# Projecting the keys of two heads at once, from rounded parts, in a latent attention kernel

## What is computed

```python
def mla(q_lat, kv_lat, k_rope, positions, q_norm_g, w_qb, kv_norm_g, w_kvb):
    q = (rms_norm(q_lat, q_norm_g) @ w_qb).reshape(bsz, s, MLA_HEADS, QK_NOPE + QK_ROPE)
    kv = (rms_norm(kv_lat, kv_norm_g) @ w_kvb).reshape(bsz, s, MLA_HEADS, QK_NOPE + V_HEAD)
    k_nope, v = kv[..., :QK_NOPE], kv[..., QK_NOPE:]
    ...
    k_pe = apply_rope(k_rope, cos, sin)
    ...
    k_full = jnp.concatenate([k_nope, jnp.broadcast_to(k_pe[:, :, None, :], ...)], axis=-1)
    out = causal_attention(q_full, k_full, v)
```

## Time and profile before

| | us |
|---|---|
| median of 3 runs (2299.27 to 2305.75) | 2302.62 |
| profiled execution, its own time | 2304.09 |
| span of that execution, first to last instruction | 2302.1 |
| TensorE busy | 2217.9 |
| VectorE busy | 1410.8 |
| GpSimd busy | 1114.1 |
| ScalarE busy | 960.9 |

### The profile page before, as it was taken

The page is one execution under the profiler, slowest core; times in us unless marked ns, Lnnn a source line. Parts: engine busy times, 40 slices in busy tenths (PEclk is TensorE's granted clock), DMA queues, the critical chain, the costliest instruction groups (busy, mean ns, idle before and its releaser), DMA issues.

```text
span 2302.1 us, 29018 instructions
## 1 busy us (share of the span) xinstructions
PE 2217.9 (96%) x10159; PEld 1806.5 (78%) x10159; DVE 1410.8 (61%) x2088; ACT 960.9 (42%) x1725; POOL 1114.1 (48%) x753
## 2 busy tenths in 40 slices
PE   8999999999999999999999999999999999999997
PEld 6786777878788888778888878878777888877886
DVE  6956655257666667697651115663876767677855
ACT  5636555124444444434531114451444444453343
POOL 2314333424577777544634322224346777764442
PEclk9999999999999999999999999999999999999998
DMA  5100000302132322664321110021123222238332
GB/s 180 46 19 1 1 0 28 128 28 97 69 119 88 111 95 81 238 199 115 92 103 62 46 37 28 28 101 55 31 84 119 87 115 84 111 136 292 95 94 91
DMA packets 66303, 203.34 MB, mean 88 GB/s; under 512 B 7360, under 2 KB 7488, under 8 KB 63104
## 3 DMA queue, kind: packets, MB, share of 16 engines
q1 hardware_dynamic: 63296, 187.19, 23.8%
q10 hardware_dynamic: 2880, 14.49, 1.6%
HBM read 152.89 MB, written 48.76 MB: 88 GB/s over the span
## 4 chain that ended last, share of the span: by engine, by line
PE 63%; DVE 14%; POOL 11%; ACT 5%; issue 5%; DMA 1%; ACTq 0%; POOLq 0%; SPq 0%; DVEq 0%
PE ps L853 9%; PE ps L855 9%; PE ps L854 9%; PE ps L985 6%; PE ps L989 6%; PE ps L987 6%; POOL wlo L644 5%; DVE ps L1226 4%; ACT ps L1043 2%; PE ps L1635 2%; POOL piece L653 2%; POOL stage L655 2%; POOL s_tmp L659 2%; DVE ps L1228 2%; PE ps L920 1%
## 5 line engine op out<-in xcount | busy, mean ns | idle before, releaser
L853 PE MATMUL ps<-ahi,whi 128*128 128x512 f32 x960 | 394.7, 411 | 14.1 <-DVE alo L2354 9.9
L566 POOL TENSOR_TENSOR whi<-stage,cons 128x1024 fp32r<-128x1024 f32 x64 | 125.3, 1958 | 527.3 <-PE ps L855 321.3
L855 PE MATMUL ps<-ahi,wlo 128*128 128x512 f32 x960 | 376.9, 393 | 0.0
L854 PE MATMUL ps<-alo,whi 128*128 128x512 f32 x960 | 376.9, 393 | 0.0
L644 POOL TENSOR_TENSOR wlo<-stage,whi 128x512 fp32r<-128x512 f32 x144 | 193.9, 1358 | 177.5 <-ACT whi L1086 177.5
L644 POOL TENSOR_TENSOR wlo<-A,whi 128x512 fp32r<-128x512 f32 x132 | 180.8, 1373 | 198.6 <-ACT whi L1096 198.6
L985 PE MATMUL ps<-x_hi,whi 128*128 128x512 f32 x616 | 244.0, 396 | 16.7 <-DVE hT L1359 9.6
L920 PE MATMUL ps<-ahi,whi 128*128 128x512 f32 x576 | 227.5, 395 | 15.7 <-ACT upg L1127 13.2
L989 PE MATMUL ps<-x_hi,wlo 128*128 128x512 f32 x616 | 242.2, 393 | 0.0
L987 PE MATMUL ps<-x_lo,whi 128*128 128x512 f32 x616 | 242.1, 393 | 0.0
L853 PEld LDWEIGHTS ps<-ahi,whi 128*128 128x128 f32 x960 | 182.2, 190 | 57.0 <-issue 18.3
(11 more groups left out here) (331 smaller groups left out, 4553.2 us busy)
## 6 DMA issues: line engine op xcount, KB each, us to landing
stage<-in_wt SPq DMA_DIRECT2D x140, 512.0 KB, 3.5
hops<-hs SPq DMA_DIRECT2D x22, 1792.0 KB, 5.7
x_late<-hops SPq DMA_DIRECT2D x132, 256.0 KB, 2.7
A<-in_wt SPq DMA_DIRECT2D x88, 256.0 KB, 4.7
x_early<-hops SPq DMA_DIRECT2D x22, 256.0 KB, 4.6
hT<-in_xt SPq DMA_DIRECT2D x16, 256.0 KB, 7.5
hT<-in_xt ACTq DMA_DIRECT2D x8, 512.0 KB, 8.1
spill<-hT ACTq DMA_DIRECT2D x1, 4096.0 KB, 12.6
```

Source lines behind the costliest of these rows:

```text
L566: nc.gpsimd.tensor_tensor(whi[:, slot, :], stage[:, st, :], one_col.to_broadcast([P, 1024]), ALU.mult).then_inc(w_hi, 1)
L853: nc.tensor.matmul(bank, hi, rhs_k[0][:, tok], start=k_first, stop=False)
L854: nc.tensor.matmul(bank, hi, rhs_k[1][:, tok], start=False, stop=False)
L855: return nc.tensor.matmul(bank, lo, rhs_k[0][:, tok], start=False, stop=k_last)
```

## The change

- Keys of a pair are projected together, with the 128 key columns of both its heads, and only in steps 2 and 3 of a pair's second half, for the next pair (`project_keys`). First halves project queries only.
- That product is made from rounded parts: `wk_hi`, `wk_lo` for the weights, `key_hi`, `key_lo` for the latents, three products for each half of the tokens. GpSimd splits the latents once (`key_latents`, behind head 1's split) and the weights' low part for each pair (`key_weight_rest`); ScalarE rounds the weights (`key_weights`) in step 4 of a first half.
- Heads 0 and 1 get their keys from the two unrounded products ahead of the loop, which now have 128 weight columns instead of 64 (`wk_first`).
- The odd head's keys have a buffer of their own, `kf[1]`. ScalarE copies each product twice, PSUM rows 0 to 63 to `kf[0]` and rows 64 to 127 to `kf[1]`; VectorE copies the shared rotated rows into `kf[1]` once.
- TensorE waits for both copies of the first pair ahead of the first scores, and for both copies of a slot before the next product in the bank. GpSimd gets two waits ahead of the weights that follow attention.

```diff
-        kf = at("kf", sh + 53 * KB, [P, S])
+        kf = [at("kf0", sh + 53 * KB, [P, S]), at("kf1", 28 * KB, [P, S])]
...
-        wk = at("wk", x0 + 36 * KB, [P, 2, NOPE])
+        wk_hi = at("wk_hi", x0 + 36 * KB, [P, 2, NOPE], F32R)
+        wk_lo = at("wk_lo", x0 + 36 * KB + 512, [P, 2, NOPE], F32R)
+        wk_first = at("wk_first", x0 + 36 * KB + 512, [P, 2 * NOPE])
+        key_hi = at("key_hi", 12 * KB, [P, S], F32R)
+        key_lo = at("key_lo", x0 + 8 * KB, [P, S], F32R)
...
+            def key_weight_rest(pair):
+                pool.wait_ge(sem("wk_in"), pair + 1)
+                nc.gpsimd.tensor_tensor(wk_lo[:], wkvb_s[:, pair * 2 * P:(pair + 1) * 2 * P]
+                                        .rearrange("p (n c) -> p n c", n=2)[:, :, 0:NOPE],
+                                        wk_hi[:].bitcast(F32), ALU.subtract).then_inc(sem("key_parts"), 1)
+
+            def key_latents():
+                pool.wait_ge(sem("v_mm"), TT)
+                nc.gpsimd.tensor_tensor(key_hi[:, :], lat[:, 2, :], one_col.to_broadcast([P, S]), ALU.mult
+                                        ).then_inc(sem("key_parts"), 1)
+                pool.wait_ge(sem("key_parts"), 1)
+                nc.gpsimd.tensor_tensor(key_lo[:, :], lat[:, 2, :], key_hi[:, :].bitcast(F32), ALU.subtract
+                                        ).then_inc(sem("key_parts"), 1)
...
+                if h == 1:
+                    key_latents()
+                if h % 2 and h + 1 < HEADS:
+                    key_weight_rest(h // 2 + 1)
+            pool.wait_ge(sem("proj"), projected(2, 1, 3))
+            pool.wait_ge(sem("qk_lo"), 4 * HEADS)
...
+            def project_keys(p, s):
+                if s == 0:
+                    pe.wait_ge(sem("key_parts"), 2)
+                    pe.wait_ge(sem("key_parts"), p + 3)
+                    pe.wait_ge(sem("q_turned"), p * 4 + 6)
                 else:
-                    pe.wait_ge(sem("q_turned"), h * 2 + part)
...
-                    mm = nc.tensor.matmul(ps[0:NOPE, bank, :], wk[:, par, :], lat[:, 2, tok], start=True, stop=True)
-                mm.then_inc(sem("proj"), 1)
+                    pe.wait_ge(sem("k_nope"), p * 4 + 6)
+                hi, lo = (w[:, :, :].rearrange("p n c -> p (n c)") for w in (wk_hi, wk_lo))
+                nc.tensor.matmul(ps[:, 0, :], hi, key_hi[:, halves[s]], start=True, stop=False)
+                nc.tensor.matmul(ps[:, 0, :], hi, key_lo[:, halves[s]], start=False, stop=False)
+                nc.tensor.matmul(ps[:, 0, :], lo, key_hi[:, halves[s]], start=False, stop=True
+                                 ).then_inc(sem("proj"), 1)
...
-                    if k < 4 and not (last and par == 1):
-                        project(p * 2 + par + 1, 1 - par, k)
+                    if k < 2 and not (last and par == 1):
+                        project_queries(p * 2 + par + 1, 1 - par, k)
+                    if k in (2, 3) and par == 1 and not last:
+                        project_keys(p, k - 2)
...
+            pe.wait_ge(sem("k_nope"), 4)
             for i in range(2):
                 scores(0, 0, i, i)
...
-                    if k < 4 and not (last and par == 1):
-                        nope(p * 2 + par + 1, k)
+                    if k < 2 and not (last and par == 1):
+                        query_nope(p * 2 + par + 1, k, 0, projected(p, par, k))
+                    if k in (2, 3) and par == 1 and not last:
+                        for odd in range(2):
+                            key_nope(k - 2, odd, 0, projected(p, 1, k))
...
             first_query_hi(1, 0)
+            act.wait_ge(w_used, T_L0_OUT)
+            for s in range(2):
+                key_nope(s, 1, first_banks[2 + s], s + 1)
             values_out(7)
...
+            dve.wait_ge(sem("kpe_ready"), 1)
+            nc.vector.tensor_copy(kf[1][a32, :], kf[0][a32, :]).then_inc(sem("kpe_ready"), 1)
```

More of the change, by code:

```diff
@@ L310, in build, with keys_copied, projected @@
         first_banks = (7, 4, 2, 3)
+        def keys_copied(h, s):
+            return 2 * (h % 2) + s + 1 if h < 2 else 4 * (h // 2) + 2 * s + h % 2 + 1
+        def projected(p, par, n):
+            return p * 6 + (4 + 2 * par + n + 1)
         def groups_of(qt):
@@ L1561, in values, with project_queries @@
                                  start=True, stop=True).then_inc(sem("v_mm"), 1)
[L1563 to L1567, removed]
+            def project_queries(h, par, s):
+                if s == 0:
+                    pe.wait_ge(sem("wh_in"), h)
                     pe.wait_ge(sem("wh_rest"), h)
                     pe.wait_ge(sem("dve_lat"), 4)
-                if part in (0, 3):
-                    pe.wait_ge(sem("k_nope"), h * 2 + part // 3)
-                else:
-                    pe.wait_ge(sem("q_turned"), h * 2 + part)
[L1574 to L1583, removed]
-                    mm = nc.tensor.matmul(ps[0:NOPE, bank, :], wk[:, par, :], lat[:, 2, tok], start=True, stop=True)
-                mm.then_inc(sem("proj"), 1)
@@ new lines, in project_queries @@
+                pe.wait_ge(sem("q_turned"), h * 2 + s)
+                for k in range(2):
+                    wc = slice(k * P, (k + 1) * P)
+                    nc.tensor.matmul(ps[:, 0, :], wh_hi[:, par, wc], lat_hi[:, k, halves[s]], start=(k == 0), stop=False)
+                    nc.tensor.matmul(ps[:, 0, :], wh_hi[:, par, wc], lat_lo[:, k, halves[s]], start=False, stop=False)
+                    mm = nc.tensor.matmul(ps[:, 0, :], wh_lo[:, par, wc], lat_hi[:, k, halves[s]], start=False,
+                                          stop=(k == 1))
@@ L1594, in project_first @@
                 else:
-                    mm = nc.tensor.matmul(ps[0:NOPE, bank, :], wkvb_s[:, 0:NOPE], lat[:, 2, tok], start=True, stop=True)
+                    mm = nc.tensor.matmul(ps[:, bank, :], wk_first[:, :], lat[:, 2, tok], start=True, stop=True)
                 mm.then_inc(sem("proj"), 1)
@@ L2086, in first_key_hi @@
                 act.wait_ge(w_ready, T_L0_OUT + 1)
-                nc.scalar.copy(k_hi[0][0:QK, halves[s]], kf[0:QK, halves[s]]).then_inc(sem("qk_hi"), 1)
+                nc.scalar.copy(k_hi[0][0:QK, halves[s]], kf[0][0:QK, halves[s]]).then_inc(sem("qk_hi"), 1)
             def first_query_hi(n, s):
```

59 lines of the change are left out of this document (36 added, 23 removed).

## The result

| | us, median (range) | mean granted clock of the runs |
|---|---|---|
| before | 2302.80 (2299.08 to 2305.75) | 0.9896 |
| changed | 2307.78 (2305.04 to 2310.41) | 0.9859 |

The times are of ten runs each, side by side; the clock of before is that of all its 123 runs in this study for which a clock is recorded. The ratio is 1.0024, interval 1.0014 to 1.0033. Forecast were 2299.5 us and a range of 2295 to 2304: wrong in sign and outside the range, though the difference is still within the 0.3% that was called no change. The interval leaves out 1, so there is a loss to explain.

What follows compares the result with a forecast made beforehand. TensorE, 96% busy, was taken to bound the kernel, beside a chain of TensorE, VectorE and ScalarE in attention. -4.08 + 0.54 + 0.45 = -3.1 us against the median 2302.62 gave 2299.5 us, range 2295 to 2304.

Steps and rivals of the forecast that it cites:

- First halves, -1.02 each: Four first halves lose both key slots: exp 4 to copy of step 4 from 3.53 to 2.51 us, 4.08 us gained.
- Second halves, +0.18 each: Three second halves: ScalarE's doubled key copies make exp 5 start 0.18 us late, 0.5 us lost in all.
- The price for the upper partitions: Second halves: a ScalarE copy from the upper 64 partitions might take double, 3 x 1.5 = 4.5 us; 0.48 a copy was taken.
- Start, +0.45: Before the first scores: head 1's two copies delay them 0.97 us, of which only 0.45 shows behind VectorE's earlier work.
- VectorE's copy, GpSimd, ScalarE's casts, 0: VectorE's 32x1024 copy at the start, GpSimd's splits and ScalarE's 128x128 casts in first halves: hidden, no time added.
- rival C: TensorE's clock falls in new idle time of the changed halves: +8.8 us, 2311.4 us if in all seven; 5%.
- pair two: Second pair of heads in the loop: same idle stretches at full clock, used as evidence against clock falls.
- the group of three: Second halves' key slot: three rounded products take 0.80 us instead of 1.01 for the unrounded one.
- the place of the new waits on ScalarE: TensorE waits for head 1's copies before the first scores; in second halves, for both first-slot copies before the second group, costing nothing.
- rival A: Whole kernel: all 9.3 us taken off TensorE come back, giving 2293.3 us; 10%.

Runs made afterwards that it cites:

- e14: Changed kernel with head 1's first key copies early and idle products at the start, in first halves and in the turns of second halves: 2299.65 us, ratio 0.9987.
- e8: Kernel before, with first halves' key products and copies cut to 8 of 512 columns: 2300.87 us, ratio 1.0002.
- e4: Changed kernel with the scaling of output 1 moved ahead of the rotation's last op on VectorE in first halves: 2305.39 us, ratio 1.0025.
- e11: Kernel before, with six idle products in the second half of each pair but the last, around the weighings of steps 5 and 7: 2300.30 us, ratio 0.9992.
- e7: Changed kernel without ScalarE's copies of the odd head's keys in second halves: 2306.44 us, ratio 1.0029.
- e3: Kernel before, with two more ScalarE copies ahead of the last values copy and TensorE waiting for them before the first scores: 2302.87 us, ratio 1.0005.
- e13: Changed kernel with six idle products in the second half of each pair but the last, as in e11: 2307.27 us, ratio 1.0022.
- e2: Changed kernel with eight idle products ahead of the first scores: 2303.66 us, ratio 1.0012.
- e5: Changed kernel with two idle products in each of steps 2 and 3 of first halves: 2305.37 us, ratio 1.0017.
- e9: Changed kernel with head 1's first copies early, five idle products before the first scores and 3, 2, 2 in steps 2 to 4 of first halves: 2303.39 us, 1.0004.
- e6: Kernel before, with five idle products ahead of the first scores: 2302.51 us, ratio 1.0000.
- e12: Kernel before, with each ScalarE key copy of second halves made twice: 2302.53 us, ratio 0.9997.
- e1: Changed kernel with head 1's two first key copies on ScalarE moved behind the first two copies of values: 2306.79 us, ratio 1.0024.
- e10: Kernel before with first-half key work cut as in e8, plus two idle products ahead of each cut product: 2302.40 us, ratio 1.0002.

## Why the prediction was wrong

**The sum of the path.** Within the kernels (290 runs, a common slope), time rises by 0.68 us for each us of lost clock. At equal lost clock (24 us) the kernel before stands at 2301.7, the changed one at 2302.1, e14 at 2302.3. So by its path the change is worth about nothing, where I had -3.1. The terms, from parts of the loop without a fall (exp of a 1024-wide step to that of the 640-wide, and on to the next 1024-wide):

- *First halves, -1.02 each: mis-sized, half of it.* The key part went from 13.79 to 13.25 us, -0.54 (the last from 13.98 to 13.36), and e8, with nothing but the key work cut, gives -0.52. The step that failed is the reading of the earlier trace rows: the last half has no keys, but it has no rotation of queries either, so it couldn't show output 1 late behind the rotation. I had even noted that maximum 4 stands behind the rotation; output 1 stands between them, and TensorE needs it for bank 7. e4, with output 1 out of the way, has the forecast 1.02 us in this part (1.06). The part before is 0.1 us longer in the second and third pair (11.82 to 11.90), 0.04 in the first, and the same in the last. There ScalarE starts on the first queries 0.53 us after the start of their last product, not 0.43 (308.38 to 308.91; before 307.90 to 308.33), and TensorE then waits 0.19 us for the rotation. The register waits are my guess for that 0.1: the last pair, written out without registers, has neither the wait nor the longer part, but no run tests it. Together -2.0 instead of -4.08.
- *Second halves, +0.18 each: mis-sized.* The first part went from 11.57 to 12.27 us (+0.70), the second from 17.08 (e11) to 16.70 (e14) (-0.38): +0.32 net, +1.0 for three. The copies are 0.61 apart, not 0.48, and the 0.2 us of the shorter group don't show: with one copy (e7) the first part is 11.62, as before. The price for the upper partitions that I feared (double) isn't there; the spacing grew for both copies, and what of it is the form and what the waits stays open.
- *Start, +0.45: about right.* Where the clock didn't fall at once, VectorE waited 0.53 (e3) to 0.72 us (e13) for the first scores.
- *VectorE's copy, GpSimd, ScalarE's casts, 0: right.* GpSimd's busy time rose by 4.7 us in the first pair and 0.5 in the others, and no rows of TensorE name it as releaser there.

So -2.0, +1.0 and +0.5 to +0.7 make -0.5 to -0.3, against +0.4 at equal clock from the runs, with a standard error of about 0.4. Neither is far from nothing, and neither is -3.1.

**The clock.** The rest is rival C, to which I gave 5%: 8.5 us more lost clock x 0.68 = 5.8 us, and the means over all runs differ by 6.2 (2307.9 against 2301.7). Two things were wrong in how I priced it. First, the condition: I let it count from six new falls at 1.7 us on, one in each changed half. In attention the changed kernel's trace has only two falls that the one before lacks, 3.4 us at the start and 1.7 at 302; larger ones behind a first half, up to 6.8 us, stand in the traces of its variants (e2, e7, e13). Which of them its own slower runs had isn't known, since one run was profiled, the fastest. Second, I argued against it from pair two, which had the same idle stretches at full clock; but the change makes just these stretches emptier, so what they were before was no evidence. The Trainium skill, "TensorE: Matmul & The Clock Gate", section "What's actually happening", was quoted in the prediction as a rule that can speak against a gain; it does here: e7 and e13 show the order of events, and in e2, e5, e9 and e14 more work for TensorE meant less time.

Where the lost clock belongs is known only roughly. Filling the start of the changed kernel returned 5.6 of the 8.5 us (e2), filling the first halves 2.9 (e5), both at once with the early copies 7.4 (e9); the controls e6 and e12 moved nothing. From the other side, the late start laid on the kernel before costs 2.7 (e3) and the cut first halves 2.8 (e8). Each figure has a standard error of 0.8 to 1.5 us, so that they add up to the 8.5 or not says little. And they don't all fit: e1 took the longer gap at the start away and returned 1.0 us, where e2, which filled that gap with products, returned 5.6. So the gap's length isn't the whole of what e2 repaired; what else it was isn't known, and e2's own trace still has falls at 194 and 210 us. e10's filling returned nothing that can be told. What is shown is that the clock is the cause and that fillings in all places together win it back; the share of each place stays open. Nor is it settled why in e13 filled turns were followed by larger falls in the first halves.

**Right in the prediction:** the group of three in 0.80 us, the place of the new waits on ScalarE, the hidden work of VectorE and GpSimd, and rival A's refusal: 9.3 us less for TensorE, no time of it returned.

## What to carry to other kernels

Work taken out of a nearly full TensorE is worth nothing where it leaves a hole that another engine fills late; look for what the removed work had been hiding, first of all who must read a PSUM bank before it is written again, and take for comparison only a stretch in which the other engines do the same. Add up the granted clock of all runs, not of one profile, before you explain a difference of a few tenths of a per cent by instructions. Where a change thins a stretch, try idle products in it: if the time falls with more work, it was the clock.

## What the hardware showed that I had not expected

- The granted clock falls in a kernel with TensorE 96% busy, and in steps: the full-rate work missing in one fall was 1.7, 3.4, 5.1 or 6.8 us in all 16 traces, the last 20 us of the span left out.
- The same thin stretch of TensorE (1.41, 1.54 and 1.30 us busy in three stretches of 2 us) was followed by a fall of 6.8 us in e7 and by none in the changed kernel's trace.
- A long fall goes on through full work: in e7 TensorE was busy without a gap from 214 to 224 us, at 0.50.
- One us of lost clock costs 0.68 us of time, not one; presumably TensorE would have waited for other engines in the rest, which no run shows.
- Two copies of 64x512 on ScalarE in a row took 1.07 us at the start of the changed kernel and 1.19 in its loop; what stood behind them started after 1.09 and 1.22.
